# Two transformer blocks on one core: other rounds of the first modulation product, and gate rows from a product with ones

## What is computed

```python
shift, scale, gate = split(silu(c) @ w_ada + b_ada, 3)          # c: one row of 2048
shift_c, scale_c, _ = split(silu(c_ctx) @ w_ada + b_ada, 3)
hc = rmsnorm(ctx, g_pre) * (1 + scale_c) + shift_c              # 256 context tokens
hx = rmsnorm(x, g_pre) * (1 + scale) + shift
zc, zx = hc @ w_in[:, :XBC_W + DT_W], hx @ w_in                 # then conv, SSD, MLP mix
out = rmsnorm(mix_out(...) @ w_out, g_post)
x = x + gate * out
```

## Time and profile before

| what | us |
| --- | --- |
| median of 3 runs | 1934.46 |
| profiled execution | 1933.41 |
| its span, first to last instruction | 1931.4 |
| PE busy | 1898.6 (98%) |
| DVE busy | 1233.7 (64%) |
| ACT busy | 976.8 (51%) |
| GpSimd (POOL) busy | 100.5 (5%) |

### The profile page before, as it was taken

How to read it: one execution, slowest core, us unless ns; L and a number is a source line. 1 busy time by engine, 2 the same in 40 slices (tenths; PEclk the granted TensorE clock), 3 DMA queues, 4 the chain that set the end, 5 groups by cost and what they waited for, 6 DMA issues and landing times.

```text
span 1931.4 us, 28815 instructions
## 1 busy us (share of the span) xinstructions
PE 1898.6 (98%) x11080; PEld 1603.8 (83%) x11080; DVE 1233.7 (64%) x1740; ACT 976.8 (51%) x1414; POOL 100.5 (5%) x107
## 2 busy tenths in 40 slices
PE   6999999999999999999999999999999999999999
PEld 3677888988888777878879988888889999998887
DVE  4547555784568898767766677566555555455554
ACT  3233322455455766754345434576454565656642
POOL 0010000000023432000000000000000000000000
PEclk9999999999999999999999999999999999999999
DMA  9953222466665675768865455545555555555564
GB/s 391 416 184 109 89 88 87 131 207 200 182 188 183 186 203 171 238 205 304 304 220 168 145 163 161 167 139 158 186 181 182 168 176 167 170 168 162 172 186 162
DMA packets 173005, 360.54 MB, mean 187 GB/s; under 512 B 11552, under 2 KB 26096, under 8 KB 167760
## 3 DMA queue, kind: packets, MB, share of 16 engines
q1 hardware_dynamic: 163616, 349.36, 56.1%
q10 hardware_dynamic: 8928, 8.47, 1.9%
q0 software_dynamic: 336, 0.98, 0.1%
HBM read 356.61 MB, written 2.16 MB: 186 GB/s over the span
## 4 chain that ended last, share of the span: by engine, by line
PE 92%; DVE 3%; DMA 2%; ACT 1%; issue 1%; SPq 0%; DVEq 0%; ACTq 0%
PE acc L630 54%; PE acc L617 15%; PE acc L593 12%; DMA raw_first<-in_ada_units 2%; PE side L683 1%; PE side L851 1%; PE side L593 1%; PE side L978 1%; DVE conv L2027 1%; PE side L905 1%; PE side L840 1%; DVE w_lo L1842 1%; PE side L752 1%; ACT w_hi L1190 1%; PE side L1114 0%
## 5 line engine op out<-in xcount | busy, mean ns | idle before, releaser
L1842 DVE TENSOR_TENSOR w_lo<-raw,w_hi 128x1024 fp32r<-128x1024 f32 (+1 forms) x551 | 670.3, 1222 | 418.8 <-ACT w_hi L1190 412.9
L1190 ACT CAST w_hi<-raw 128x1024 fp32r<-128x1024 f32 (+1 forms) x544 | 561.0, 1036 | 604.1 <-PE acc L630 395.6
L630 PE MATMUL acc<-w_hi,h_hi 128*128 128x512 f32 (+1 forms) x1312 | 521.4, 397 | 2.5 <-DVE h_lo L2220 1.8
L630 PE MATMUL acc<-w_hi,h_lo 128*128 128x512 f32 (+1 forms) x1312 | 509.4, 388 | 0.0
L630 PE MATMUL acc<-w_lo,h_hi 128*128 128x512 f32 (+1 forms) x1312 | 508.8, 388 | 0.0
L630 PEld LDWEIGHTS acc<-w_hi,h_hi 128*128 128x128 f32 x1312 | 246.9, 188 | 52.9 <-DVE h_lo L2220 2.1
L630 PEld LDWEIGHTS acc<-w_hi,h_lo 128*128 128x128 f32 x1312 | 246.6, 188 | 51.2
L630 PEld LDWEIGHTS acc<-w_lo,h_hi 128*128 128x128 f32 x1312 | 247.1, 188 | 46.5
L617 PE MATMUL acc<-h_hi,w_hi 128*128 128x256 f32 x896 | 258.1, 288 | 1.0 <-DVE h_lo L2220 1.0
L617 PE MATMUL acc<-h_lo,w_hi 128*128 128x256 f32 x896 | 254.8, 284 | 0.0
L617 PE MATMUL acc<-h_hi,w_lo 128*128 128x256 f32 x896 | 254.7, 284 | 0.0
(11 more groups left out here) (389 smaller groups left out, 1951.3 us busy)
## 6 DMA issues: line engine op xcount, KB each, us to landing
raw<-in_w_in SPq DMA_DIRECT2D x176, 512.0 KB, 4.4
raw<-in_w_in_odd SPq DMA_DIRECT2D x128, 512.0 KB, 3.7
raw<-in_w_in_even SPq DMA_DIRECT2D x96, 512.0 KB, 3.7
raw<-in_w_out SPq DMA_DIRECT2D x64, 512.0 KB, 5.5
raw_first<-in_ada_units SPq DMA_DIRECT2D x29, 1024.0 KB, 15.8
gate_w<-in_gate_units SPq DMA_DIRECT2D x32, 512.0 KB, 6.5
raw<-in_w_out_even SPq DMA_DIRECT2D x32, 512.0 KB, 4.7
raw<-in_w_out_odd SPq DMA_DIRECT2D x32, 512.0 KB, 4.6
```

Of the source, the lines that this page charges most:

```text
L630: o = nc.tensor.matmul(ACC[b][:, 0:n], l, r, start=first and kk == 0 and m == 0, stop=last and kk == 1 and m == 2)
L1190: act.copy(WHI[:, u % 4, :, 0:n], RAW[:, u % 4, :, 0:n]).then_inc(hi_ready, 1)
L1842: dve.tensor_tensor(WLO[:, u % 4, :, 0:n], RAW[:, u % 4, :, 0:n], WHI[:, u % 4, :, 0:n].bitcast(F32), ALU.subtract).then_inc(lo_ready, 1)
```

## The change

It has three parts.

1. **Rounds.** The modulation comes in 9 rounds: rounds 0 and 1 have one feature block and two `ada` units each (eight products of 256 columns in a unit), rounds 2 to 8 two blocks and four units. Loads follow that order, with unit 0 of `w_in` ahead of `ada` units 2 and 3. On PE, unit 2 has the first two `ada` units of round 3 between its banks, later even units have the last `ada` unit of a round after their first bank, and the transposes of round 3 lie in unit 3.
2. **Squares.** `x_squares` writes four buffers instead of two; `x_reduce` adds a second time (to a quarter); each sum takes two products instead of four; root and reciprocal are taken for ctx and x apart.
3. **Gate.** `gate_mac` starts from the bias, which a DMA of GpSimd puts into `gate_sum` (one of two buffers; 256 KB a time, rows of zeros but for one), and GpSimd loads `g_post` into `gate_bc` spread over partitions (1 MB). One product with ones of 512 columns does sum and spreading, and DVE multiplies the result with `g_post`. ACT's copy, `gate_sum` and `gate_col_out` go.

```diff
+ROUNDS = 9
+ada_kts = lambda r: (r,) if r < 2 else (2 * r - 2, 2 * r - 1)
+ada_first = lambda r: 2 * r if r < 2 else 4 * r - 4
+ada_units = lambda r: 2 if r < 2 else 4
+LOADS = []
+for _r in range(ROUNDS):
+    LOADS += [("ada", _r, v) for v in range(ada_units(_r))]
+    LOADS += [("w", 0, m) for m in ((_r,) if _r < 2 else (2 * _r - 2, 2 * _r - 1))]
+EARLY, RING = 2, 7
...
             def x_sums(i):
                 pe.wait_ge(xss_ok, i + 1)
-                for k in range(4):
+                for k in range(2):
+                    o = nc.tensor.matmul(ACC[1 + i // 2][:, 0:SEQ], ONE[:], SQX[i][:, k, :],
...
+            ada(0, 0)
+            ada(0, 1)
+            ada_turn(0)
+            pe.wait_ge(xrow_ok, 2)
+            pe.wait_ge(w0_half, 2)
+            early(0, (0,))
+            ada(1, 0)
+            ada(1, 1)
+            ada_turn(1)
+            ada(2, 0)
+            early(0, (1,))
+            for v in range(1, 4):
+                ada(2, v)
+            ada_turn(2)
+            early(1)
+            early(2, mid={1: lambda: (ada(3, 0), ada(3, 1))})
+            ada(3, 2)
+            ada(3, 3)
+            early(3, mid={0: lambda: ada_turn(3)})
+            for r in range(4, ROUNDS):
+                for v in range(3):
+                    ada(r, v)
+                early(2 * r - 4, mid={0: lambda: ada(r, 3)})
+                ada_turn(r)
+                early(2 * r - 3)
+            early(14)
+            early(15)
...
-            def gate_sum(q):
...
-            def gate_rows(b):
+            def gate_rows(q):
                 pe.wait_ge(gate_used, q * 8 + 8)
+                nc.tensor.matmul(SB[q][:], con("one"), GAC[:, q % 2, :], start=True, stop=True).then_inc(gg_done, 1)
...
-            def gate_row_out(b):
-                act.wait_ge(gg_done, b + 1)
-                act.copy(GG[:, b * NCOL:(b + 1) * NCOL], SB[b][:]).then_inc(gg_ok, 1)
...
             def x_reduce(i):
+                q = SQX[i]
+                seq(dve.tensor_tensor(q[:, 0:4], q[:, 0:4], q[:, 4:8], ALU.add))
+                dve.tensor_tensor(q[:, 0:2], q[:, 0:2], q[:, 2:4], ALU.add).then_inc(xss_ok, 1)
+            def x_invert(a):
+                dve.wait_ge(nrt_ok, a + 1)
+                dve.reciprocal(RBX[:, a, :], RBX[:, a, :]).then_inc(xrow_ok, 1)
...
             def gate_mac(n):
                 if n % 8 == 0:
-                    if n:
-                        dve.wait_ge(gsum_done, n // 8)
+                    dve.wait_ge(gac_in[q % 2], 16 * (q // 2) + 16)
...
-            def gate_col_out(q):
...
+            def gate_row_out(q):
+                s_ = slice(q * NCOL, (q + 1) * NCOL)
+                dve.wait_ge(bc_in, 80)
+                dve.wait_ge(gg_done, q + 1)
+                dve.tensor_tensor(GG[:, s_], SB[q][:], GG[:, s_], ALU.mult).then_inc(gg_ok, 1)
...
             w0_lo(1)
+            x_scale(1)
+            first_lo(1)
+            ada_out(1)
+            mod(1)
             x_mod(1)
             halve(1)
             x_scale(2)
             x_scale(3)
+            for p in range(1, UPC):
+                if p > 1:
+                    first_lo(2 * p - 1)
+                ada_out(p + 1)
+                mod(p + 1)
+                if p < 7:
+                    x_scale(2 * p + 2)
+                    x_scale(2 * p + 3)
+                for kt in (2 * p, 2 * p + 1):
                     x_mod(kt)
                     halve(kt)
+                first_lo(2 * p)
             first_lo(15)
...
+            pool.wait_ge(y_ok, 8)
+            for q in range(4):
+                if q >= 2:
+                    pool.wait_ge(gg_done, q - 1)
+                pool.dma_start(GAC[:, q % 2], dram["gate_bias"][q]).then_inc(gac_in[q % 2], 16)
+                if q == 0:
+                    pool.dma_start(GG[:], dram["g_post"][0].partition_broadcast(P)).then_inc(bc_in, 16)
             pool.wait_ge(h_turned, 32)
```

More of the change, by code:

```diff
@@ L681, in ada @@
                 pe.wait_ge(ada_in[ada_slot(n)], ada_uses(n) * 16)
-                for j in range(4):
-                    o = nc.tensor.matmul(ada_bank(e)[32 * j:32 * j + 32, :], SC[:, 4 * v + j, :], ada_raw(n)[:, j],
-                                         start=v == 0, stop=v == AW4 - 1, tile_position=(0, 32 * j))
+                wide = 4 * len(ada_kts(e))
+                w = ada_raw(n).rearrange("p j h n -> p (j h n)").rearrange("p (j n) -> p j n", n=64 * wide)
+                nj = 32 // wide
+                for j in range(nj):
+                    o = nc.tensor.matmul(ada_bank(e)[32 * (j % 4):32 * (j % 4) + 32, 0:64 * wide], SC[:, nj * v + j, :], w[:, j],
+                                         start=v == 0 and j < 4, stop=v == ada_units(e) - 1 and j >= nj - 4,
+                                         tile_position=(0, 32 * (j % 4)))
                 o.then_inc(ada_used, 1)
@@ L689, in ada_turn @@
                 pe.wait_ge(ada_ok, e + 1)
-                for k in range(4):
+                for k in range(2 * len(ada_kts(e))):
                     o = nc.tensor.transpose(ada_bank(e)[:, k * P:(k + 1) * P], ADR[:, e % 2, k * P:(k + 1) * P], con("ident"))
@@ L696, in x_sums @@
                 pe.wait_ge(xss_ok, i + 1)
-                for k in range(4):
-                    o = nc.tensor.matmul(ACC[1][:, i // 2 * SEQ:(i // 2 + 1) * SEQ], ONE[:], SQX[i % 2][:, k, :],
-                                         start=i == 0 and k == 0, stop=i % 2 == 1 and k == 3, skip_group_check=True)
+                for k in range(2):
+                    o = nc.tensor.matmul(ACC[1 + i // 2][:, 0:SEQ], ONE[:], SQX[i][:, k, :],
+                                         start=i % 2 == 0 and k == 0, stop=i % 2 == 1 and k == 1)
@@ L700, in x_sums, with early @@
                 o.then_inc(xsum_done, 1)
+            def early(m, kks=range(2), mid={}):
+                pe.wait_ge(h_ok, m // 2 * 2 + kks[-1] + 1)
+                done = unit("BD" if m % 2 else "B0", 0, m // 2, 0, m == 1 or kks[0] == 0 and m == 0, m >= 14, m=m, kks=kks, mid=mid)
+                if kks[-1]:
+                    done[-1][1].then_inc(unit_used, 1)
             for i in range(4):
                 x_sums(i)
[L705 to L720, removed]
@@ L1201, in x_squares, with x_root @@
                 act.wait_ge(xt_in[i], 16)
[L1202 to L1210, removed]
+                act.activation(SQX[i][:], XT[:, i // 2, i % 2 * 8:i % 2 * 8 + 8, :], ACT.Square).then_inc(nsq_ok, 1)
+            def x_root(a):
+                act.wait_ge(xsum_done, 2 * a + 2)
+                act.activation(RBX[:, a, :], ACC[1 + a][:, 0:SEQ], ACT.Sqrt, scale=1.0 / D, bias=STAT[:, 63:64]).then_inc(nrt_ok, 1)
             def modulate(kt):
                 act.wait_ge(xr_ok, kt + 1)
[L1215 removed]
+                act.wait_ge(mod_ok, kt // 2 + 2 if kt > 1 else kt + 1)
                 for a in range(2):
@@ L1314, in _ @@
                 x_squares(i)
[L1315 to L1322, removed]
+            x_root(0)
+            x_root(1)
+            act.wait_ge(raw_in[0], 16)
+            act.copy(WHI[:, 0, 0, :], RAW[:, 0, 0, :]).then_inc(w0_half, 1)
+            act.copy(WHI[:, 0, 1, :], RAW[:, 0, 1, :]).then_inc(hi_ready, 1)
+            modulate(0)
+            first_hi(1)
+            modulate(1)
+            for e in range(1, UPC):
+                first_hi(2 * e)
                 modulate(2 * e)
@@ L1912, in gate_mac @@
                 for kk in range(2):
[L1913 to L1917, removed]
+                    o = dve.scalar_tensor_tensor(GAC[:, q % 2], GS[:, n % 3, kk, :], vec("c", 2 * (n % 8) + kk), GAC[:, q % 2],
+                                                 ALU.mult, ALU.add)
                     if kk == 0:
@@ L1958, in _ @@
                 x_reduce(i)
-            x_invert()
+            x_invert(0)
+            x_invert(1)
             x_scale(0)
-            x_scale(1)
             ada_out(0)
```

102 lines of the change are left out of this document (33 added, 69 removed).

## The result

| | before | after |
| --- | --- | --- |
| median of 5 runs | 1934.37 us | 1942.89 us |
| range | 1932.78 to 1934.78 | 1940.72 to 1943.57 |
| profiled execution | 1933.41 us | 1940.72 us |
| its span | 1931.4 us | 1938.8 us |

The change makes the kernel slower: the ratio is 1.0041 (95% interval 1.0028 to 1.0054), 8.5 us between the medians and 7.3 us between the two profiled executions (that of after is the fastest of its five). The forecast was 1935.1, and 1942.89 lies above its range.

The account below looks back on a forecast made before the run. PE was taken to bound the kernel (92% of the chain), with transfers full too. First stretch +3.8 and gate -3.2 gave +0.6 us on 1934.46, so 1935.1 us; range 1930.4 to 1938.2.

Parts of the forecast that it names:

- To unit 2: From the inputs' copy to unit 2's first product: unit 2 starts at 49.2 us, 2.3 us earlier than before.
- The inputs' path: Squares, sums and root up to round 0's copy: the copy starts 4.1 us sooner, at 22.8 us.
- this doubt: On the inputs' last sum: TensorE's clock may stay low, gaining 0.1 and not 1.0 us; copy starts at 23.7.
- DVE's 6.0: Ahead of unit 2, DVE needs 6.0 us for factors, two scalings, two blocks and the next `w_lo`.
- The upper bound, 51.1: Latest start of unit 2, with the low clock in the sums and unit 0: 51.1 us.
- Low clocks after 33 us: Sign against the forecast: it is wrong if TensorE's granted clock is low after 33 us.
- Rival (b): TensorE stays at 1.2 GHz from the sums to unit 1: +9.6 us in sum, 1944.1 us, slower; chance 0.07.
- Putting them between banks costs nothing in itself: From unit 2 to B1: `ada` units placed between banks of even units add 0 us by their place.
- The waits at units 4 and 14: Moves leave DVE's work uncovered: PE waits +1.0 us at unit 4 and +1.5 at unit 14.
- The gate: On PE's chain in O1, each of four gate rows loses the 0.79 us for sums: -3.2 us.
- Queues: New waits and DMA queues: bias lands at 775.7 to 777.5, before 778.8, costing 0 us, range 0 to 2.
- a load late in S: Sign against the forecast: SP's loads in phase S might land up to an estimated 3.3 us later.

Follow-up runs that it names:

- gate_only: The kernel before with only the gate part of the change (GpSimd's DMAs, one product with ones per gate row); 1931.77 us, ratio 0.9985.
- old_order: Changed kernel, nine rounds kept, but all four `ada` units ahead of each even unit and the last transposes inside unit 12, as before; 1935.4 us, ratio 0.9999.
- sq_gate: The kernel before with the squares and gate parts of the change, its rounds and order kept; 1931.5 us, ratio 0.9982.
- not_inside: The changed kernel with every `ada` unit ahead of its even unit and none between banks; 1941.44 us, ratio 1.0032.
- inside_only: The kernel before with the last `ada` unit of rounds 2 to 6 moved behind the first bank of units 2, 4, 6, 8 and 10; 1935.08 us, ratio 1.000.
- last_turn: The changed kernel with round 8 alone in the old order: four `ada` units ahead of unit 12, last transposes inside it; 1939.31 us, ratio 1.0025.
- old_warm: `old_order` with 12 and 7 extra identity products in PE's pauses ahead of unit 0's halves; 1932.23 us, ratio 0.9985.
- warm_small: The changed kernel with 12 and 7 extra identity products in PE's pauses ahead of unit 0's halves; 1940.55 us, ratio 1.0028.

## Why the prediction was wrong, step by step

| step | predicted | measured |
| --- | --- | --- |
| unit 0's first product | 26.9 | 26.71 |
| its two halves | 4.5 and 2.7 us | 5.09 and 4.61 |
| unit 2 against before | -2.3 | +1.07 |
| four more `ada` units behind it | +3.6 | +3.57 |
| wait at unit 4 | +1.0 | +1.27 |
| wait at unit 14 | +1.5 | +2.02 |
| `ada` units between banks | 0 | +2.38 |
| B1 against before | +3.8 | +10.31 |
| the gate | -3.2 | -3.8 |
| sum | +0.6 | +6.5 |

The waits are counted from starts, with the slower first product behind them; PE's idle time was 1.10 and 1.85. The 2.38 are what is left of 10.31 after the other four terms; five rounds at 0.34 to 0.38 and 0.34 in unit 2 are 2.1 of them, and the rest lies in units 3 and 13. From the sum of 6.5 to the shift of the last product, 7.1, it is +1.6 for a stretch at the low clock in O1 (granted 0.66 from 880 to 885; `gate_only` and `old_order` show one too, `sq_gate` doesn't), and -1.0 later. Two steps failed: "To unit 2", in the second half's clock, and the place of the `ada` units, taken as free.

**The inputs' path** was right within 0.2 us in this trace, with some luck: its last sum took 1.13 us here, while `old_order`, with the same list up to there, took 2.07 for it, and unit 0 began at 27.21. The prediction had named this doubt.

**To unit 2** failed. The step saw that PE pauses ahead of the first half, took 4.5 us for it from the old trace, and then costed the second half at the high level, though a pause (factors, `h_hi`, `h_lo`) stood in its own working there too. The half took 4.61: 1.9 of the 3.3 us lie here. The first half adds 0.6 (less the 0.2 by which it began sooner), the hand-over to the second 0.5, and those from there to unit 2 the other 0.4. DVE's 6.0 from the transposes' end was right (46.35 to 52.34). The upper bound, 51.1, has the same gap: it adds 0.9 for the sums and 0.9 for the first half, and nothing for the second. With 5.4 for that one too, by the same rows, it would have been some 53.7. Low clocks after 33 us were among the prediction's own signs of being wrong. Rival (b) named this mechanism, but on the whole stretch and with all `ada` units at the low level; these ran at the high one (1.91 us for two), so its 1944.1 is near the result by another road (its +7.0 is 6.7, moreover, from 58.2 less 51.47).

**"Putting them between banks costs nothing in itself"** was wrong: `not_inside` and `inside_only` put it at 0.35 us each, from both sides. The step counted instructions by their mean in a row of equals, and a change of kind has a price. Six products, one `ada` unit, 18 products take 1.58 + 1.00 + 4.32 = 6.90 us in after, 5.67 + 0.89 = 6.56 apart. The `ada` products have tiles of 128 by 32, their neighbours 128 by 128. The Trainium skill, "TensorEngine Tiling (Array Packing)", section "Key Properties", says that changing the tiling mode drains TensorE; the price seen here fits it, and the rule, which gives no figure, was not weighed in the prediction. An interruption as such costs far less: in the trace of before the starts of the products around four transposes, on tiles of 128 by 128, lie 0.46 us further apart than others, 0.02 more than the transposes' row has; around one `ada` unit in after it is 1.22, 0.33 more than its 0.89. No run changed the tile shape alone.

**The waits at units 4 and 14** were the right mechanism and a size too small. At unit 14 the transposes' end to `w_lo` took 5.4 us against 5.2, and PE stood 1.85 with a slower first product behind it; `last_turn` removed all of it. That no wait came in rounds 4 to 7 was right ("still covered").

**The gate** was right and a little better than said. The chain's rows give 4 x 0.82 = 3.3. The rest is in starts: the products of O1 on either side lie 0.93 us further apart for the sums (not 0.79) and 0.91 for the spreading, and 0.88 for the new product, so a row gains 0.96 and four gain 3.8.

**Queues** were right in part. DVE came to the first `gate_mac` of after at 784.89, as late against before as the whole trace (+10.25), so the bias held nothing up. But of the two `w_lo` behind it, which wait for ACT as in the earlier trace rows, the second has to wait through ACT for a load of `w_in`, and that load stands in the chain:

```profile
784.89 1.54 DVE L1911 SCALAR_TENSOR_TENSOR gate_sum<-gate_w,vec_t,gate_sum 128x512 f32<-128x512 f32 x2
790.53 2.54 DVE L1838 TENSOR_TENSOR w_lo<-raw,w_hi 128x1024 fp32r<-128x1024 f32 x2 [4.10 <-ACT w_hi L1198]
```

```profile
780.75 9.99 DMA raw<-in_w_in
790.76 1.06 ACT w_hi L1198
```

PE's wait for `w_lo` there is 0.8 us in after against 0.6 before, 1.4 in `gate_only` and 1.6 in `last_turn`; in `sq_gate` and `old_warm` it stays at 0.6. So a load late in S, a sign of being wrong by the prediction's own words, did come, at a price of 0.2 here and up to 1.0 elsewhere. The rule of the Trainium skill on queues taken in turn ("DMA: Bandwidth & Descriptors", section "Queues, rings and completion order") would make SP's loads later in this way; that it is the cause is not shown, since no run took GpSimd's transfers away by themselves.

**What stays open:** why the clock falls behind one wait of 1.9 us and not behind another of the same length at the same place (unit 14: 5.71 us in after, 7.33 in `not_inside`). Nor is the first half of unit 0 alike in kernels with the same list up to there: 4.5 us in before (granted 0.68 from 30 to 35), 2.97 in `inside_only` (1.00). The pause is shown to go with it, not to be enough.

## What to carry to other kernels

Work that another engine must finish before the next unit needs cover on the bounding engine, so count for each moved instruction what it covered and not just what it costs: transposes that came 1.6 us later, and last ones with no `ada` unit behind them, opened waits of 1.3 and 2.0 us. Keep instructions of one kind together on TensorE, or price each change of kind from a row of the trace. A wait on TensorE can have a second price behind it in the clock, so ask where the next wait stands: of 2.9 us gained ahead of unit 2 nothing was left at B1 in `warm_small`, where waits followed, and 2.7 stayed in `old_warm`, where none did.

## What was not expected of the hardware

- An `ada` unit (tiles of 128 by 32) between full products costs 0.34 to 0.38 us beyond its 0.89.
- The clock can fall some products into a unit and not at once: in `not_inside` the first products of unit 14 start 0.23 to 0.31 us apart (134.83 to 136.06), the next ones 0.43 (136.41 to 139.40), and then 0.23 again.
- A float32 product of 128 columns counts as two instructions and takes some 0.12 us for each (24 in 2.84, 48 in 5.52 us).
